# A two-block f32 transformer on one core: halves of normed heads exchanged by on-chip DMA copies in place of permutation products, with moves in the MLP, index, ride and value-copy steps

## The reference, cut to what matters

```python
def apply_rope(z, cos, sin):
    half = z.shape[-1] // 2
    z1 = z[..., :half].astype(jnp.float32)
    z2 = z[..., half:].astype(jnp.float32)
    c, s = cos[:, None, :], sin[:, None, :]
    return jnp.concatenate([z1 * c - z2 * s, z2 * c + z1 * s], axis=-1).astype(z.dtype)
...
    y = rms_norm(x, norm_g) @ w_in
    qa, ka, va, qi, ki, wi, za, qb, kb, vb, zb = split_cols(y, AB_SPLITS)
...
    qa = apply_rope(rms_norm(heads(qa, A_HEADS), a_qk_norm[0]), cos, sin)
    ka = apply_rope(rms_norm(heads(ka, A_KV_HEADS), a_qk_norm[1]), cos, sin)
    qi = apply_rope(qi.reshape(bsz, seq, IDX_HEADS, IDX_DIM), icos, isin)
    ki = apply_rope(rms_norm(ki, a_kidx_norm)[:, :, None, :], icos, isin)[:, :, 0]
...
def apply_rope_2(x, ang):
    xf = x.astype(jnp.float32).reshape(x.shape[:-1] + (HEAD_DIM // 2, 2))
    cos = jnp.cos(ang)[None, :, None, :]
    sin = jnp.sin(ang)[None, :, None, :]
    x1, x2 = xf[..., 0], xf[..., 1]
    out = jnp.stack([x1 * cos - x2 * sin, x1 * sin + x2 * cos], axis=-1)
    return out.reshape(x.shape).astype(x.dtype)
```

## Time and profile before

| | |
|---|---|
| median of 3 runs | 3815.56 us (3815.26 to 3815.78) |
| the profiled execution | 3819.4 us |
| its span in the trace | 3817.5 us |
| mean granted clock of TensorE | 0.993 of full |
| TensorE busy | 3710.2 us, 97% |
| VectorE busy | 2044.7 us, 54% |
| ScalarE busy | 965.0 us, 25% |
| GpSimd busy | 553.3 us, 14% |
| moved by DMA | 349.84 MB, mean 92 GB/s |

### The profile page before, as it was taken

One profiled execution on the slowest core, in us unless ns is written; L12 is line 12 of the kernel. 1 busy time (PEld: TensorE's weight loads), 2 busy tenths in 40 slices (PEclk: granted clock), 3 DMA queues, 4 the chain that ended last, 5 costly groups with the idle time before them and its releaser, 6 DMA issues.

```text
span 3817.5 us, 42943 instructions
## 1 busy us (share of the span) xinstructions
PE 3710.2 (97%) x16520; PEld 2581.6 (68%) x16520; DVE 2044.7 (54%) x3524; ACT 965.0 (25%) x2229; POOL 553.3 (14%) x480
## 2 busy tenths in 40 slices
PE   9999999999999999999999899999999999999999
PEld 4458445555654555555678678888568888878887
DVE  3654345735674566554523946664775666344343
ACT  2142214621453212112200732020312111212020
POOL 1001000001000111111221511111002111211112
PEclk9999999999999999999999999999999999999999
DMA  3112332022001233332342314443202454112221
GB/s 137 63 45 90 102 88 79 1 79 88 26 1 34 76 110 111 111 132 100 102 129 90 83 45 154 168 163 110 89 22 89 157 185 162 65 67 89 89 89 45
DMA packets 231113, 349.84 MB, mean 92 GB/s; under 512 B 32321, under 2 KB 100577, under 8 KB 230881
## 3 DMA queue, kind: packets, MB, share of 16 engines
q1 hardware_dynamic: 205712, 328.99, 25.2%
q0 software_dynamic: 6816, 10.01, 1.3%
q10 hardware_dynamic: 18384, 8.11, 0.7%
HBM read 341.42 MB, written 4.06 MB: 90 GB/s over the span
## 4 chain that ended last, share of the span: by engine, by line
PE 90%; DVE 6%; ACT 2%; issue 2%; ACTq 0%; POOL 0%; DMA 0%; DVEq 0%; POOLq 0%
PE psum L1893 48%; PE psum L1634 26%; PE psum L2013 3%; PE psum L1960 3%; PE psum L1990 2%; DVE small L2990 2%; PE psum L1742 1%; DVE arena L2651 1%; ACT arena L2393 1%; PE psum L1663 1%; PE psum L1675 1%; PE psum L1692 1%; ACT arena L2381 1%; PE psum L1581 1%; DVE psum L2986 0%
## 5 line engine op out<-in xcount | busy, mean ns | idle before, releaser
L1634 PE MATMUL psum<-HC,ring 128*128 128x256 f32 (+1 forms) x2928 | 922.3, 473 | 7.1 <-issue 3.9
L1634 PEld LDWEIGHTS psum<-HC,ring 128*128 128x128 f32 x2928 | 549.7, 190 | 363.5 <-issue 310.6
L1893 PE MATMUL psum<-arena,ring 128*128 128x256 f32 (+1 forms) x2368 | 619.3, 415 | 5.2 <-ACT arena L2147 5.2
L1893 PEld LDWEIGHTS psum<-arena,ring 128*128 128x128 f32 x2368 | 445.6, 190 | 151.2 <-ACT arena L2147 10.0
L1893 PE MATMUL psum<-arena 128*128 128x256 f32 (+1 forms) x1984 | 516.1, 414 | 0.4
L2523 DVE TENSOR_TENSOR arena<-psum,arena 128x384 f32<-128x384 f32 (+2 forms) x332 | 182.9, 558 | 578.8 <-PE psum L1893 577.5
L1893 PE MATMUL psum<-HC,ring 128*128 128x256 f32 (+1 forms) x1984 | 479.0, 395 | 5.1 <-ACT arena L2147 4.4
L1893 PEld LDWEIGHTS psum<-arena 128*128 128x128 f32 x1984 | 376.9, 190 | 120.2 <-ACT arena L2152 0.7
L1893 PEld LDWEIGHTS psum<-HC,ring 128*128 128x128 f32 x1984 | 374.5, 190 | 86.3 <-ACT arena L2147 5.1
L3129 POOL TENSOR_TENSOR ring<-ring 128x1024 f32<-128x1024 f32 (+1 forms) x86 | 237.7, 2764 | 1330.3 <-DVE arena L2461 1254.3
L2651 DVE SCALAR_TENSOR_TENSOR arena<-ring,cond,arena 128x512 f32<-128x512 f32 x448 | 318.6, 749 | 8.0
(11 more groups left out here) (246 smaller groups left out, 3608.2 us busy)
## 6 DMA issues: line engine op xcount, KB each, us to landing
ring<-in_mlp_w SPq DMA_DIRECT2D x64, 2048.0 KB, 8.8
ring<-in_ada_w SPq DMA_DIRECT2D x48, 2048.0 KB, 7.9
ring<-in_na_qkv SPq DMA_DIRECT2D x10, 2048.0 KB, 8.1
ring<-in_ab_in SPq DMA_DIRECT2D x5, 2048.0 KB, 8.3
ring<-in_cd_in SPq DMA_DIRECT2D x4, 2048.0 KB, 10.2
ring<-in_pw SPq DMA_DIRECT2D x8, 1024.0 KB, 6.8
ring<-in_at_qkv SPq DMA_DIRECT2D x3, 2048.0 KB, 10.3
ring<-in_ab_out SPq DMA_DIRECT2D x2, 2048.0 KB, 7.7
```

What stands on the lines that cost most here:

```text
L1634: last = nc.tensor.matmul(out, lhs, rhs, start=(k == 0), stop=(k == len(t.pairs) - 1))
L1893: last = nc.tensor.matmul(bank(at, u["T"], u["T"] * m), still, moving, start=(opens and m == 0 and i == 0), stop=(i == k - 1), skip_group_ ...
```

## The change

Six edits in one:

1. **Swap.** `swap` on TensorE now makes only the products of the two unnormed QI tiles. For every normed head ScalarE, at its "spread" step (which it had none of before), waits for VectorE's scaled `yn` and issues DMA copies of `yn` back into the head's own tile with the halves exchanged: 4 copies of 32 partitions, 8 of 16 for `quad`, 2 of every second partition for the attention layer of block 2. VectorE's rotation waits for them and multiplies in place. The list of the second layer moves `qc` 2 and 3 from tile 20 to tile 23 and `ksw` to the front of tile 37's list.
2. **Index.** The index block's products are made from x times the norm's gain (XG), before and around the first norm's sums, and VectorE multiplies them by the reciprocal root as it takes them out of PSUM. The block's weights are loaded in four pieces between those of x. 4 products on constants are left of 14; GpSimd adds the squares of k = 1 to 6; ScalarE's tables are issued behind its squares. The side steps of the top-k and the spreads stand later in the first layer's list.
3. **Joint MLP.** Products 1 and 2 of the second unit stand behind the first two of the first; `cnorm` is moved from the last tile of the stage before to behind product 1.
4. **The MLPs after it.** The sum t[0] is made in a low and a high half, and product 5 waits for each.
5. **Ride.** The group that carries modulation weights in the second layer has one tile, KR, where it had KR and Z2[5]; that tile goes to the next group.
6. **Value copies.** The six shifts are issued by GpSimd behind the gate of the attention stage.

```diff
-                       summed=KD - 1 if stages else KD // 2, strips=strips, to=to or (H, CH), early=early)
+                       summed=KD - 1, strips=strips, to=to or (H, CH), early=early)
...
+        XG = dsa_wk[:, 0:KD * S].rearrange("p (t s) -> p t s", s=S)
+        rstd_wide = dsa_wk[:, KD * S:KD * S + S]
         idx_b = block(dram["ab_in"][:, 0:IDX_COLS].rearrange("(k p) n -> p k n", p=P))
-        idx_tiles = [t_tile(idx_b, KD, P * j, P, H, S, "act", "copy", dst)
+        idx_tiles = [t_tile(idx_b, KD, P * j, P, XG, S, "dve", "by_rstd", dst, 1.0)
                      for j, dst in ((2, KI[:, 0]), (0, QI[:, 0]), (1, QI[:, 1]))]
-        wi_rows = QA[0:4, 0, :]
-        wi_made = t_tile(idx_b, KD, 3 * P, 4, H, S, "act", "scale", wi_rows, 1.0 / 16)
+        wi_rows = QA[0:4, 3, :]
+        wi_made = t_tile(idx_b, KD, 3 * P, 4, XG, S, "dve", "by_rstd", wi_rows, 1.0 / 16)
+        raw_tiles = [*idx_tiles, wi_made]
+        for t, at in zip(raw_tiles, (3, 4, 5, 0)):
+            t.raw, t.bank = True, at
...
-        idx_tiles[2].after = [("swap", idx_heads, 0), ("swap", idx_heads, 1)]
-        wi_tiles[-1].after = [("swap", idx_heads, 2)]
         ab_list = [t for _, tiles, _ in ab_groups[1:] for t in tiles]
+        ab_groups[1][1][2:2] = wi_tiles
+        ab_list[0].after = [("mean", idx_heads, 0), ("sd", idx_heads, 0)]
+        wi_tiles[-1].after = [("spread", idx_heads, 0)]
+        ab_list[2].after = [("swap", idx_heads, 0), ("swap", idx_heads, 1), ("swap", idx_heads, 2)]
         qk_data = ([(QA[:, t], V("qa_g")) for t in range(4)] + [(KA[:, 0], V("ka_g"))]
                    + [(QB[:, t], V("qb_g")) for t in range(4)] + [(KB[:, 0], V("kb_g"))])
         qk_heads = heads([(d, g, ab_list[i]) for i, (d, g) in enumerate(qk_data)], S, pair_constants, P, *rope)
         for qt in range(1, ST):
             for h in range(4):
-                ab_list[2 * qt - 2 + h // 2].after.append(("index", qt, h))
-            ab_list[2 * qt - 1].after.append(("topk", qt, 0))
+                ab_list[2 * qt + 1 + (h // 2 if qt > 1 else 0)].after.append(("index", qt, h))
+            ab_list[2 * qt + 1 + (qt > 1)].after.append(("topk", qt, 0))
...
-                ab_list[12 + i // 2].after += [("swap", qk_heads, i - 2), ("swap", qk_heads, i - 1)]
-            ab_list[12 + i // 2].after += [("spread", qk_heads, i), ("spread", qk_heads, i + 1)]
-        ab_list[17].after += [("swap", qk_heads, 8), ("swap", qk_heads, 9)]
+                ab_list[13 + i // 2].after += [("swap", qk_heads, i - 2), ("swap", qk_heads, i - 1)]
+            ab_list[13 + i // 2].after += [("spread", qk_heads, i), ("spread", qk_heads, i + 1)]
+        ab_list[18].after += [("swap", qk_heads, 8), ("swap", qk_heads, 9)]
...
-        cd_group(b, [t_tile(b, KD, 384, P, H, S, "act", "copy", KR[:, 0]),
-                     t_tile(b, KD, 0, P, H, S, "act", "silu", Z2[:, 5])], True)
-        cd_group(b, [t_tile(b, KD, P * j, P, H, S, "act", "silu", Z2[:, 5 + j]) for j in (1, 2)])
+        cd_group(b, [t_tile(b, KD, 384, P, H, S, "act", "copy", KR[:, 0])], True)
+        cd_group(b, [t_tile(b, KD, P * j, P, H, S, "act", "silu", Z2[:, 5 + j]) for j in range(3)])
...
+        quad.half = 16
...
-        after(20, ("mean", nope, 4), ("mean", nope, 5), ("square", nope, 6), ("swap", qc, 2), ("swap", qc, 3))
+        after(20, ("mean", nope, 4), ("mean", nope, 5), ("square", nope, 6))
...
+        after(23, ("swap", qc, 2), ("swap", qc, 3))
...
-        after(37, ("square", kct, 0), ("mean", kct, 0), ("sd", kct, 0), ("swap", ksw, 0), ("swap", ksw, 1))
+        after(37, ("swap", ksw, 0), ("swap", ksw, 1), ("square", kct, 0), ("mean", kct, 0), ("sd", kct, 0))
...
+        def product_order(st):
+
+            us, ahead = st["units"], (1, 2) if st.get("ahead") else ()
+            out = [(us[0], p) for p in us[0]["order"][:2]] + [(us[1], p) for p in ahead]
+            out += [(us[0], p) for p in us[0]["order"][2:]]
+            out += [(u, p) for u in us[1:] for p in u["order"] if not (u is us[1] and p in ahead)]
+            for i, (u, p) in enumerate(out):
+                u.setdefault("at", {})[p] = 7 * us[0]["id"] + i + 1
+            return out
...
+            job.half = 1
...
-        at_o_tiles[15].after += [("csum", mlp_ctx, None), ("cnorm", mlp_ctx, None)]
+        at_o_tiles[15].after.append(("csum", mlp_ctx, None))
+        joint_first["after"] = {1: [("cnorm", mlp_ctx, None)]}
...
+                sp.dma_start(slot(idx_b, KD)[:, 2 * i:2 * i + 2, :],
+                             dram["ab_in"][2 * P * i:2 * P * i + 2 * P, 0:IDX_COLS].rearrange("(k p) n -> p k n", p=P)
+                             ).then_inc(idx_in[i], 16)
+            for b in range(1, len(used)):
...
+        def exchanged(job):
+
+            if job.half == 1:
+                return [(slice(a, P, 2), slice(1 - a, P, 2)) for a in range(2)]
+            rows = [slice(a, a + job.half) for a in range(0, P, job.half)]
+            return [(rows[a], rows[a ^ 1]) for a in range(len(rows))]
...
             def swap(job, i):
 
                 data, g, made_by = job.tiles[i]
+                if g is not None:
+                    return
                 at = job.turn_banks[job.r[i] % len(job.turn_banks)]
-                if g is not None:
-                    pe.wait_ge(yn_ready, job.sp[i] + 1)
-                    src = job.yn[:, job.r[i] % 2, 0:job.n]
-                else:
-                    pe.wait_ge(tables_in, tables_waited[0])
-                    if made_by is not None:
-                        pe.wait_ge(*made_by.done)
-                    src = data
+                pe.wait_ge(tables_in, tables_waited[0])
+                if made_by is not None:
+                    pe.wait_ge(*made_by.done)
                 open_bank(at)
-                nc.tensor.matmul(bank(at, job.n)[0:job.parts], job.swap, src, start=True,
+                nc.tensor.matmul(bank(at, job.n)[0:job.parts], job.swap, data, start=True,
...
+            def raw_products(ks):
+
+                for k in ks:
+                    pe.wait_ge(gained, k + 1)
+                    pe.wait_ge(idx_in[k // 2], 16)
+                    for t in raw_tiles:
+                        part, rows, cols = t.out
+                        lhs, rhs = t.pairs[k]
+                        last = nc.tensor.matmul(bank(t.bank, cols)[part:part + rows], lhs, rhs, start=(k == 0),
+                                                stop=(k == KD - 1))
+                        if k == KD - 1:
+                            last.then_inc(tile_ready, 1)
...
-                    for _ in range(14):
+                    for _ in range(4):
...
+                    raw_products(range(5))
...
+                    raw_products(range(5, 6))
...
+                    raw_products(range(6, KD))
...
+            def exchange(job, i):
+
+                if job.swap is None:
+                    return
+                r, data = job.r[i], job.tiles[i][0]
+                src = job.yn[:, r % 2, 0:job.n]
+                act.wait_ge(yn_ready, job.sp[i] + 1)
+                for to, of in exchanged(job):
+                    act.dma_start(data[to], src[of]).then_inc(turned_in[r % 2], 16)
+
+            side = dict(square=square, mean=nothing, sd=root, spread=exchange, swap=nothing, index=index, topk=nothing,
...
+                if "low" in which:
+                    dve.wait_ge(norm_ready, seen + k // 2)
+                    nc.vector.tensor_tensor(t[0][:, 0:k // 2], b12[:, 0:k // 2], b11[:, 0:k // 2], ALU.subtract
+                                            ).then_inc(t_low, 1)
+                if "high" in which:
+                    dve.wait_ge(norm_ready, seen + k)
+                    dve.wait_ge(t_low, n["low"] + 1)
+                    n["low"] += 1
+                    nc.vector.tensor_tensor(t[0][:, k // 2:], b12[:, k // 2:], b11[:, k // 2:], ALU.subtract
+                                            ).then_inc(t_made, 1)
...
-                    normed_scale(normed, 1, range(KD // 2 + 1))
-                    token_sums(st, us[0], (1,))
+                    normed_scale(normed, 1, range(3))
+                    token_sums(st, us[0], ("low",))
+                    normed_scale(normed, 1, range(3, KD // 2 + 1))
+                    token_sums(st, us[0], ("high",))
...
+                        elif t.op == "by_rstd":
+                            nc.vector.scalar_tensor_tensor(t.dst, src, t.arg, rstd_wide[0:rows], ALU.mult,
+                                                           ALU.mult).then_inc(dve_took, 1)
...
+                    for k in range(KD):
+                        dve.wait_ge(x_in[k // 2], 16)
+                        nc.vector.tensor_scalar(XG[:, k, :], X[:, k, :], st["gain"](k), None, ALU.mult).then_inc(gained, 1)
...
-                dve.wait_ge(swap_ready, r + 1)
                 if g is None:
+                    dve.wait_ge(swap_ready, job.moved[i])
                     dve.wait_ge(cos_ready, r + 1)
```

(16 more changed lines are left out.)

238 lines of the change are left out of this document (140 added, 98 removed).

## The result

The changed kernel takes 3794.14 us (median of 4 runs, 3789.81 to 3796.01) against 3815.41 (3814.74 to 3815.78): ratio 0.9942, 95% interval 0.9927 to 0.9957. It is faster by 21 us, where 46 were forecast and 3753 was the low and 3787 the high end: the direction was right, the size less than half. One run of `e5_value_load_held`, 4171.35 us at a mean granted clock of 0.874 where the others have 0.993 or 0.994, stands in that kernel's median (3790.98 without it) and not in its ratio.

A forecast was written before the change was run, and what follows sets the result against it. TensorE, busy 97% of the span, was taken as the bound. Gains of 18.0 + 15.7 + 4.4 + 0 + 5 + 3.0 = 46.1 us from 3815.6 gave 3769.5 us; own bounds 3762 to 3778, with rivals 3753 to 3787.

The forecast's parts named there:

- The top-k chain on VectorE: First layer: ends at 146.4 as before, reciprocal ends at 149.8, TensorE's first spread at 151.5, covered with 1.7 us in hand.
- landings over 5 us: Exchange copies: landings near 3 us expected; over 5 us would make the prediction wrong.
- Index products ahead of the norm: Start of the kernel: first ab tile at 37.8 instead of 61.58, 18.0 us gained, bounds 10 to 19.
- Swaps, first layer: First projection, 10 + 1 heads: copies' last rotations covered by two value tiles, gain 10.0 us.
- the qc term: Second layer's short tiles: ScalarE's eviction 6.8 us late beyond the four swaps saved, net +3.2 us.
- the ksw pair gains nothing: Second layer: a weight load of 5.32 us from 575.99 ends last there, so no gain.
- Swaps, attention layer: 10 heads, 9.05 us of swaps: 5.1 us gained after waits for reciprocals and ride; ends 1 and 9.
- rival (b): ScalarE becomes the bound where tiles are short, issues of 1 us: qc +9, attention layer +4, 3782 us; chance 0.16.
- rival (d): Slower: copies wait behind weight loads, landings of 10.6 us, 61 lost against 46, 3830 us; chance 0.04.
- Joint MLP: Second unit's product 2 wait: norm moved behind the first copy, two products fill in, -4.4 us; ends -2 and -6.
- ride: Second layer: VectorE's weight sums start a tile sooner, the 3.44 us wait at 491.40 and half-speed stretch go, about -5.
- Value copies: Before attention at 2094.61: 3.89 us idle falls to 0.9, -3.0 us; first reader arrives about when the last copy lands.

The follow-up runs named there:

- e5_value_load_held: Changed kernel, but the 2 MB MLP weight load issued ahead of the six value copies waits until they have landed; 3791.33 us, 0.9935 of the kernel before.
- e2: Changed kernel with only the four qc heads of the second layer swapped by TensorE products again; 3780.86 us, 0.9907 of the kernel before.
- e4: Changed kernel, but the 2 MB weight load issued at 426 us waits for the fourth qc head's rotation; 3789.03 us, 0.9929 of the kernel before.
- e1: Changed kernel with all swaps back on TensorE as permutation products, other edits kept; 3795.53 us, 0.9946 of the kernel before.
- e10: Changed kernel with the index edit alone undone, start and first layer's list as before; 3803.46 us, 0.9965 of the kernel before.
- e6: Changed kernel, all copies kept, three weight loads held back (qc, attention layer, value copies), 4-row index products paired; 3780.95 us, 0.9907 of the kernel before.
- e3: Changed kernel with every exchange copy issued by GpSimd in place of ScalarE; 3787.14 us, 0.9920 of the kernel before.

## Why the prediction was wrong, by its own steps

Four steps failed. The top-k chain on VectorE, which "does not move", ended 8.6 us later than forecast. The qc stretch lost 12.8 us where its terms had 3.2, mostly by a weight load in front of the copies, dearer issues and half speed. The attention layer's waits ate all of the 5.1 us, again behind a load. The value copies' first reader waited, and 3.0 us became 0.1. Of the prediction's signs, the first ab tile (39.7 for 38) and TensorE's busy time came as it said; landings over 5 us, its own sign of being wrong, came as well.

**Index products ahead of the norm: 18.0 forecast, 9.3 to 10.9 measured.** The start of TensorE's timeline after the change:

```profile
1.21 6.32 PE L1982 MATMUL psum<-mean_d 128*128 128x512 f32 x8 [1.21 <-DVE eps L3179]
7.36 18.59 PE L1972 MATMUL psum<-arena,ring 128*128 128x512 f32 x40
25.88 1.95 PE L2000 MATMUL psum<-mean_d,HC 128*128 128x1 f32 x16
...
39.70 7.13 PE L1685 MATMUL psum<-HC,ring 128*128 128x512 f32 x16
...
57.67 8.83 PE L1685 MATMUL psum<-HC,ring 128*128 128x512 f32 x16
...
158.42 1.20 PE L1726 MATMUL psum<-arena 64*128 64x512 f32 x4 [1.58 <-DVE arena L2905]
```

Step by step: filler to 7.4 (7.5 forecast), sums 1.8 (1.9), no half-speed stretch in 20 to 30, the first ab tile at 39.7 (37.8). The 1.9 us are mainly the term "0.86 us a raw product": forty records took 18.59, 0.93 a product. The rest fell behind that tile, in the sentence "the top-k chain on VectorE does not move". I counted its steps two tiles later in the list; most are three later. VectorE ends the first query tile's top-k at 96.6, only 1.2 us later than before, but then waits for the second one's index products, which moved from tiles 2 and 3 to tiles 5 and 6:

```profile
105.03 1.27 DVE L2949 SCALAR_TENSOR_TENSOR arena<-arena 128x384 f32<-128x384 f32 x2 [7.34 <-ACT arena L2352]
```

So the chain came 8.6 us later than I had it, the reciprocal ended at 158.4 and not at 149.8, and TensorE waited 1.58 us where 1.7 were "in hand" (the terms of that sum give 151.0 and not 151.5, so it was 1.2). Three more small waits stand for ScalarE among the moved steps: 0.15 and 0.34 us among the small transposes, and 1.08 where all four index products of the first query tile now come at one place and have two banks. And a tile of 7.1 took 8.83 at 57.67 in the traced execution, a half-speed stretch of its own; the traces of e2 and e4 do not have it.

**Swaps, first layer: 10.0 forecast, 9.4 measured** (e1; 8.3 beside the old start, 226.51 for e10's 218.18)**.** Right, with its step: the last rotations are covered by the value tiles.

**Swaps, second layer: the qc term, +3.2 forecast, +12.8 measured.** The mechanism was named and its point in the trace too; the terms were mis-sized. Two groups of eight issues took 5.06 and 5.01 us where 3.6 each was taken: 2.9 more. The 0.45 came from two of the cheapest issues of that line: nine of the fourteen of L2418 in the kernel before took 0.46 to 0.94. One landing lies on the chain, since TensorE waits for the second pair's issues and not for their landing. The forecast put 3.0 behind the last issue; without the load it is 1.4 (e4: issues end at 428.24, the second head's rotation starts at 429.64): 1.6 less. Behind the load: 4.3 more (e4). 6.8 + 2.9 - 1.6 + 4.3 = 12.4 of the 13.1 that TensorE waited (1.8 and 11.3); 0.7 stays without an owner. And the half-speed stretch after the wait: six microseconds at half speed are three lost, and the forecast had none. The quads came as forecast. At ksw the longer wait for the weight load was followed by half speed, which the sentence "the ksw pair gains nothing" left out; this tile took 7.05 us before, behind a wait of 0.25:

```profile
564.51 9.61 PE L1685 MATMUL psum<-HC,ring 128*24 128x512 f32 x16 [3.83 <-DMA ring<-in_cd_in]
```


**Swaps, attention layer: 5.1 forecast, 0.0 measured.** The forecast gave up 3.95 of the 9.05 us, 0.7 for the ride and the rest for reciprocals. Measured: 3.8 and 0.7 for reciprocals, 2.2 for the ride, and 1.7 at half speed. Its missing step was again a load in front of the copies: with it held, 6.1 us come (e6).

So rival (b), ScalarE as the bound, was right about the place and gave qc nearly its price (9 us more than forecast for 9.6), which is luck: it had issues of 1 us, those at qc took 0.51 to 0.64, and 4.3 of the 9.6 are the load's; rival (d), copies behind loads, was right as a mechanism but not in its size, since only a few copies meet a load. The forecast took each at a mean price, and the losses are not means: they come where a load is issued inside a chain.

The Trainium skill ("DMA: Bandwidth & Descriptors", Anatomy of one DMA) has a fixed 2.0 us and the bytes at 436 GB/s, told there for copies that GpSimd issues. By that rule, an estimate from the page, 64 KB take 2.15; the trace agrees for ScalarE's copies, 2.0 in the median of 68. The Trainium skill says on the same page ("DMA: Bandwidth & Descriptors", Issuing engines are not separate DMA queues) that transfers of all issuers interleave. The trace agrees only in part: after 430.5 they do, but for the 3 us before it the exchange queue got nothing.

**Joint MLP: 4.4 forecast, 4.3 measured. Fast MLPs: 0 and 0.1; ride: 5 and 5.1 (7.96 gained at 461.62, 13.03 at 501.94).** Right by their steps (the 1.8 in the first MLP are a half-speed stretch of before that is no longer there). **Value copies: 3.0 forecast, 0.1 measured.** The forecast had their first reader arrive "about where the last of them lands", and priced the difference at nothing. It was a wait of 1.74 us and then a second half-speed stretch. The load beside them was in the row that gave 10.6; the forecast used that number as the copies' own.

## What to carry to other kernels

A small copy on chip is cheap (2 us) and its issue is not (0.6 us of an engine's queue each). Count issues on the engine whose next instruction somebody waits for, and put copies where tiles are long. When copies sit inside a dependency chain, look up what the weight queue issues within the same microseconds, and hold back a load that isn't needed soon: three waits on SyncE gave nearly 13 us here (13.2 together with the paired products, which save 0.5 in the first five sets), more than half as much as the whole change. When a step is moved in a hand-written list, count the tiles in the list on both sides, and not the distance that was meant.

## What the runs showed that I had not expected

- Most landings of the 116 exchange copies took 1.9 to 2.1 us (median 2.0, shortest 1.7). Near a 2 MB load on another queue they took longer: up to 5.4 (load issued at 174.83, 2.7 us ahead of the copies), 6.4 (426.01) and 6.6 (902.50, among them). In the second case that queue moved 450 packets while theirs moved none. Holding the load took the delay away at 426 (e4) and at 902 (e6); the first was not tried.
- An issue costs ScalarE's queue 0.61 us in the median whether the copy has 32, 64 or 128 KB (0.47 to 1.85 over all 116; the longest, at 188 to 193 us, has no owner).
- VectorE's multiplication of two SBUF tiles took up to 3.69 us in place of 0.69 in e3. It is GpSimd's own products of two SBUF tiles that it lies beside, and not the issues: the ten long ones each overlap such products and end 0.6 us behind them, and one that lies beside an issue alone (503.07, issues from 503.45) took 0.69. No run takes the products away, so this is read from the overlaps only.
- Changing the number of stationary columns costs TensorE about 0.1 us: a set of raw products with 128, 128, 128 and 4 columns took 3.72 us (18.59 for five sets), four products of a tile 3.5 (7.03 for eight). With the 4-column ones in pairs (e6) the first five sets took 18.11.
- Some half-speed stretches stand in one kernel's trace and not in that of another with the same instructions there, as the one at 57.67. Each is worth 1.7 us or more, and the changed kernel's four runs lie 6 us apart; differences under 2 us between two kernels are not told apart here without more runs.
